# Attention rotations on VectorE from the projection's PSUM bank, the divisor moved into the rotary tables, factor products moved to ScalarE

## The reference, cut to what matters

```python
def apply_partial_rope(t, positions):
    ...
    x1 = tf[..., :half]
    x2 = tf[..., half:ROT_DIM]
    out = jnp.concatenate([x1 * cos - x2 * sin, x2 * cos + x1 * sin, tf[..., ROT_DIM:]], axis=-1)
```

## Time and profile before

| what | value |
|---|---|
| time, median of 3 runs | 2723.34 us (2721.16 to 2724.14) |
| the profiled execution: its own time | 2725.44 us |
| its span, first to last instruction | 2723.6 us |
| mean granted TensorE clock | 0.951 |
| TensorE busy | 2497.2 us (92%) |
| VectorE busy | 1613.0 us (59%) |
| GpSimd busy | 1659.7 us (61%) |
| ScalarE busy | 474.7 us (17%) |

### The profile page before, as it was taken

The page is one execution under the profiler, slowest core; times in us unless marked ns, Lnnn a source line. Parts: engine busy times, 40 slices in busy tenths (PEclk is TensorE's granted clock), DMA queues, the critical chain, the costliest instruction groups (busy, mean ns, idle before and its releaser), DMA issues.

```text
span 2723.6 us, 33885 instructions
## 1 busy us (share of the span) xinstructions
PE 2497.2 (92%) x11937; PEld 2018.0 (74%) x11937; DVE 1613.0 (59%) x1859; ACT 474.7 (17%) x904; POOL 1659.7 (61%) x700
## 2 busy tenths in 40 slices
PE   6998999988999989788888889999999998999997
PEld 4776767866878867677777778878878666887886
DVE  5876234775473377766666647444588565644456
ACT  4523222013000012011101111000032342100000
POOL 4334544665777756455555537787878323777784
PEclk7999999998999989899999999999999888999998
DMA  6212344221323312122222213323323111332331
GB/s 236 70 62 80 118 150 161 102 85 55 112 81 93 113 57 78 62 66 74 66 73 73 65 43 93 96 97 93 107 78 95 54 31 32 93 108 84 94 109 52
DMA packets 61230, 237.70 MB, mean 87 GB/s; under 512 B 7072, under 2 KB 12200, under 8 KB 57424
## 3 DMA queue, kind: packets, MB, share of 16 engines
q1 hardware_dynamic: 54720, 230.51, 26.6%
q10 hardware_dynamic: 6416, 5.95, 0.7%
HBM read 232.24 MB, written 2.10 MB: 86 GB/s over the span
## 4 chain that ended last, share of the span: by engine, by line
PE 76%; DVE 13%; ACT 3%; DVEq 2%; issue 2%; ACTq 1%; POOL 1%; DMA 1%; POOLq 1%
PE gg L533 17%; PE gg L534 17%; PE gg L535 17%; DVE ta L2298 2%; PE babcd L571 2%; PE babcd L573 2%; PE babcd L572 2%; PE gg L907 2%; PE gg L909 1%; PE gg L908 1%; PE babcd L533 1%; PE babcd L534 1%; PE babcd L535 1%; DVEq L2297 1%; DVE qk L2300 1%
## 5 line engine op out<-in xcount | busy, mean ns | idle before, releaser
L463 POOL TENSOR_TENSOR w_hi<-raw,zero 128x1024 fp32r<-128x1024 f32 (+2 forms) x280 | 587.6, 2098 | 687.9 <-PE gg L535 461.7
L465 POOL TENSOR_TENSOR w_lo<-raw,w_hi 128x1024 fp32r<-128x1024 f32 (+2 forms) x280 | 754.0, 2693 | 39.9
L533 PE MATMUL gg<-h_hi,w_hi 128*128 128x512 f32 x1576 | 633.2, 402 | 85.5 <-DVEq L2291 76.0
L534 PE MATMUL gg<-h_lo,w_hi 128*128 128x512 f32 x1576 | 625.2, 397 | 0.0
L535 PE MATMUL gg<-h_hi,w_lo 128*128 128x512 f32 x1576 | 624.7, 396 | 0.0
L533 PEld LDWEIGHTS gg<-h_hi,w_hi 128*128 128x128 f32 x1576 | 304.0, 193 | 161.7 <-DVEq L2291 70.2
L535 PEld LDWEIGHTS gg<-h_hi,w_lo 128*128 128x128 f32 x1576 | 302.8, 192 | 65.4
L534 PEld LDWEIGHTS gg<-h_lo,w_hi 128*128 128x128 f32 x1576 | 304.1, 193 | 62.1
L2024 DVE TENSOR_TENSOR ta<-ff_s,gg 128x512 f32<-128x512 f32 x64 | 44.1, 689 | 331.3 <-PE gg L535 323.8
L454 POOL TENSOR_TENSOR w_hi<-raw,zero 128x1536 fp32r<-128x1536 f32 (+2 forms) x48 | 107.2, 2233 | 186.7 <-PE babcd L535 142.3
L533 PE MATMUL gg<-u_hi,w_hi 128*128 128x512 f32 x528 | 209.7, 397 | 4.2 <-issue 4.2
(11 more groups left out here) (570 smaller groups left out, 3984.3 us busy)
## 6 DMA issues: line engine op xcount, KB each, us to landing
raw<-in_w_ff_in_a SPq DMA_DIRECT2D x66, 512.0 KB, 3.6
raw<-in_w_ff_in_b SPq DMA_DIRECT2D x66, 512.0 KB, 3.6
raw<-in_w_att_qk SPq DMA_DIRECT2D x48, 512.0 KB, 3.6
raw<-in_w_ff_out_a SPq DMA_DIRECT2D x24, 704.0 KB, 4.1
raw<-in_w_ff_out_b SPq DMA_DIRECT2D x24, 704.0 KB, 4.1
late_raw<-in_w_ada SPq DMA_DIRECT2D x16, 1024.0 KB, 5.0
raw<-in_w_ml SPq DMA_DIRECT2D x25, 512.0 KB, 3.6
raw<-in_w_merge_a SPq DMA_DIRECT2D x16, 768.0 KB, 5.5
```

What stands on the lines that cost most here:

```text
L463: pool.tensor_tensor(hi, a, zero[:].to_broadcast([P, size * P]), ALU.add)
L465: pool.tensor_tensor(lo, a, hi, ALU.subtract).then_inc(S["units_split"], 1)
L533: pe.matmul(dst, w_hi[slot][:, blk], xs[0][:, k, :], start=k == 0, stop=False)
L534: pe.matmul(dst, w_hi[slot][:, blk], xs[1][:, k, :], start=False, stop=False)
```

## The change

Four things change, all in the attention.

- `rotate` reads the first 32 rows from the projection's bank instead of from `qk`, and its intermediate results go to bank `bf` (shuffle, cosine product) and to `ta` (sine product). Only head 0's units 2 to 5 still read `qk`. The bank is given back (`att_copied`) by the cosine product, not by the eviction. The eviction still covers all 128 rows, and `rotate` then overwrites the first 32.
- The rotary tables are multiplied by `rstd` once, the first 32 rows of `rstd` become 1, and the second pair of tables goes away. For s below 2, the layout changes in the rotation's sum too.
- In each slot VectorE evicts and rotates unit s first, and the work for the head before comes behind it (`score` at s = 0, `swap_in` at 1, `swap_out` at 2), except `factors`, which stands ahead of unit 3's eviction. TensorE's `att_swap` moves behind unit 2 and writes to `ba`. In head 1 all of this stands one slot later.
- The eight products of `norm` move from VectorE to ScalarE, behind a new semaphore `att_factors`.

Head 0 gets other banks for its units 2 and 5, and another order of evictions.

```diff
@@ -257,12 +257,11 @@
         p_nat = at(62, "p_nat", [P, TB, 2 * P])
         p_res = at(66, "p_res", [P, 4, 2 * P])
         pt_res = at(70, "pt_res", [P, 8 * P])
-        nat_c, nat_s = sq[0][0:32, :], sq[1][0:32, :]
         sel_in = at(95, "sel_in", [P, P])
         sel_out = at(95.5, "sel_out", [P, P])
         rope_c, rope_s = at(80, "rope_c", [32, SEQ]), at(112, "rope_s", [32, SEQ])
         a0, a1, a2 = (at(83 + 2 * i, f"phase{i}", [32, SEQ])[:] for i in range(3))
-        ra = [ta[0:32, :], tb[0:32, :]]
+        ra = ta[0:32, :]
         a_st = at(82, "a_st", [P, 96])
         swap_y = at(82.5, "swap_y", [P, 2, 32])
         swap_m = at(82.875, "swap_m", [P, 2, 4])
@@ -614,7 +613,7 @@
 
                 pe.wait_ge(S["colv_ready"], nth)
                 for b in range(TB):
-                    mm = pe.matmul(bank[:, b:b + 1], rstd[:, b * P:(b + 1) * P], ident[:, 0:1], start=True, stop=True)
+                    mm = pe.matmul(bank[:, b:b + 1], rstd[:, b * P:(b + 1) * P], ident[:, 64:65], start=True, stop=True)
                 mm.then_inc(S["rows_ready"], 1)
 
             def residual(name, kb, xs, nth, shift=False, lead=None, **first):
@@ -1001,9 +1000,7 @@
                 if s < 2:
                     return
                 ready(u0 + s)
-                if s == 5:
-                    pe.wait_ge(S["att_copied"], 2)
-                cols_mm((bf[:], ba, bb, g[1])[s - 2], (u0 + s) % 2, 8, (h_hi, h_lo))
+                cols_mm((bc, ba, bb, bd)[s - 2], (u0 + s) % 2, 8, (h_hi, h_lo))
                 if s == 3:
                     sum_rows(SQ["att"])
                 if s == 5:
@@ -1036,8 +1033,8 @@
                 y = swap_y[:, 0, :].rearrange("p (x r) -> p x r", x=8)
                 for b in range(TB):
                     rows = slice(32 * b, 32 * b + 32)
-                    pe.matmul(bf[rows, 0:8], sel_in[:, rows], y[:, b:8:4, :], start=True, stop=True)
-                pe.matmul(bf[:, 8:40], sel_out[:], swap_y[:, 1, :], start=True, stop=True).then_inc(S["att_swapped"], 1)
+                    pe.matmul(ba[rows, 0:8], sel_in[:, rows], y[:, b:8:4, :], start=True, stop=True)
+                pe.matmul(ba[:, 8:40], sel_out[:], swap_y[:, 1, :], start=True, stop=True).then_inc(S["att_swapped"], 1)
             def att_turn(a):
 
                 for bank, first, last, rows in ((ba, 0, 4, 3), (bb, 4, 7, 4)):
@@ -1070,7 +1067,7 @@
 
                 if s == at_step:
                     att_scores(a, p)
-                if s == at_step + 1:
+                if s == at_step + 2:
                     att_swap(a)
                 if s == 5:
                     att_turn(a)
@@ -1083,7 +1080,7 @@
                             first_head(s)
                             continue
                         project(h, s)
-                        att_step(h - 1, 1 - p, s, 2 * isinstance(h, int))
+                        att_step(h - 1, 1 - p, s, int(isinstance(h, int)))
                     project_values(h, 0)
                     if not first:
                         att_values(h - 1, 1 - p)
@@ -1557,6 +1554,11 @@
             def shifts(a):
                 wait(act, "att_shift", a + 1)
                 act.activation(a_st[:, 40:56], a_st[:, 40:56], ACT.Exp).then_inc(S["att_fexp"], 1)
+            def norm(a):
+                wait(act, "att_factors", a + 1)
+                for n in range(8):
+                    part = p_nat[:, n, nat_part(n)] if n < 4 else p_res[:, n - 4, :]
+                    act.activation(part, part, ACT.Copy, scale=a_st[:, 72 + n:73 + n]).then_inc(S["att_norm"], 1)
             def turned(a):
                 wait(act, "att_values", a)
                 for n, bank in enumerate((ba, bb[:, 0:3 * P], bc, bd)):
@@ -1566,6 +1568,7 @@
             def att_head(a):
                 expo(a)
                 shifts(a)
+                norm(a)
                 turned(a)
             def att_two(i):
                 for p in range(2):
@@ -2275,30 +2278,47 @@
             layer_norm(1, scaled_tile, "att")
             for k in range(KD):
                 add_square(SQ["att"], k)
-            rows_inverse(3)
+            wait(v, "std", 3)
+            v.reciprocal(rstd[:], rstd[:])
             wait(v, "att_consts", 64)
-            v.tensor_copy(by_token(nat_c), by_residue(rope_c[:]))
-            v.tensor_copy(by_token(nat_s), by_residue(rope_s[:]))
             v.drain()
+            v.tensor_tensor(rope_c[:], rope_c[:], rstd[0:32, :], ALU.mult)
+            v.tensor_tensor(rope_s[:], rope_s[:], rstd[0:32, :], ALU.mult)
+            v.drain()
+            v.memset(rstd[0:32, :], 1.0)
+            v.drain().then_inc(S["colv_ready"], 1)
+            def first_bank(s):
+                return (g[0], g[1], bc, ba, bb, bd)[s]
             def projection_out(h, p, s):
 
                 wait(v, "units_used", h * 8 + (FIRST["w_att"] + s + 1))
-                bank = (g[0], g[1], bf[:], ba, bb, g[1])[s] if isinstance(h, int) and h == 0 else g[s % 2]
+                first = isinstance(h, int) and h == 0
+                bank = first_bank(s) if first else g[s % 2]
                 if s < 2:
                     v.tensor_tensor(by_token(qk[p][:, s, :]), by_residue(bank), by_residue(rstd[:]), ALU.mult)
                 else:
-                    v.tensor_tensor(qk[p][:, s, :], bank, rstd[:], ALU.mult)
-                v.drain().then_inc(S["att_copied"], 1)
+                    out = v.tensor_tensor(qk[p][:, s, :], bank, rstd[:], ALU.mult)
+                    if first:
+                        out.then_inc(S["att_copied"], 1)
+                v.drain()
             def rotate(h, p, s):
                 q = qk[p][0:32, s, :]
-                cosine, sine = (nat_c, nat_s) if s < 2 else (rope_c[:], rope_s[:])
-                v.stream_shuffle(ra[0], q, SWAP16)
-                v.tensor_tensor(ra[1], q, cosine, ALU.mult)
-                v.drain()
-                v.tensor_tensor(ra[0], ra[0], sine, ALU.mult)
-                v.drain()
-                v.tensor_tensor(q, ra[0], ra[1], ALU.add)
-                v.drain().then_inc(S["att_roped"], 1)
+                from_qk = isinstance(h, int) and h == 0 and s > 1
+                src = q if from_qk else g[s % 2][0:32, :]
+                turn = bf[0:32, :]
+                v.stream_shuffle(turn, src, SWAP16)
+                v.drain()
+                v.tensor_tensor(ra, turn, rope_s[:], ALU.mult)
+                v.drain()
+                part = v.tensor_tensor(turn, src, rope_c[:], ALU.mult)
+                if not from_qk:
+                    part.then_inc(S["att_copied"], 1)
+                v.drain()
+                if s < 2:
+                    v.tensor_tensor(by_token(q), by_residue(turn), by_residue(ra), ALU.add).then_inc(S["att_roped"], 1)
+                else:
+                    v.tensor_tensor(q, turn, ra, ALU.add).then_inc(S["att_roped"], 1)
+                v.drain()
             def score(a):
 
                 wait(v, "att_turned", a * 4)
@@ -2325,10 +2345,10 @@
             def swap_out(a):
 
                 wait(v, "att_swapped", a + 1)
-                v.tensor_copy(a_st[:, 24:32], bf[:, 0:8])
+                v.tensor_copy(a_st[:, 24:32], ba[:, 0:8])
                 picked = swap_y[:, 1, :].rearrange("p (s r b) -> p s r b", s=2, r=4)
                 for n in range(2):
-                    v.tensor_tensor(picked[:, n, :, :], bf[:, 8 + 16 * n:24 + 16 * n].rearrange("p (r b) -> p r b", r=4),
+                    v.tensor_tensor(picked[:, n, :, :], ba[:, 8 + 16 * n:24 + 16 * n].rearrange("p (r b) -> p r b", r=4),
                                     swap_m[:, 0, :].unsqueeze(2).to_broadcast([P, 4, 4]), ALU.mult)
                 v.drain()
                 tt(picked[:, :, 0:2, :], picked[:, :, 0:2, :], picked[:, :, 2:4, :], ALU.add)
@@ -2346,12 +2366,8 @@
                 tt(eight(64), eight(56), eight(64), ALU.add)
                 v.reciprocal(a_st[:, 64:72], a_st[:, 64:72])
                 v.drain()
-                tt(a_st[:, 72:80], a_st[:, 40:48], a_st[:, 64:72], ALU.mult)
-            def norm(a):
-
-                for n in range(8):
-                    part = p_nat[:, n, nat_part(n)] if n < 4 else p_res[:, n - 4, :]
-                    v.tensor_scalar(part, part, a_st[:, 72 + n:73 + n], None, ALU.mult).then_inc(S["att_norm"], 1)
+                v.tensor_tensor(a_st[:, 72:80], a_st[:, 40:48], a_st[:, 64:72], ALU.mult)
+                v.drain().then_inc(S["att_factors"], 1)
             def head_out(a):
                 wait(v, "att_values", a + 1)
                 hi, lo = (pick(o, a) for o in (o_hi, o_lo))
@@ -2363,50 +2379,33 @@
                 for p in range(2):
                     h = i * 2 + p
                     if isinstance(h, int) and h == 0:
-                        for s in range(6):
+                        for s in (2, 3, 4):
                             projection_out(h, p, s)
-                        for s in range(6):
+                        projection_out(h, p, 0)
+                        rotate(h, p, 0)
```

(42 more changed lines are left out.)

## The result

| | before | after |
|---|---|---|
| median | 2723.45 us (2721.16 to 2724.14, 4 runs) | 2640.71 us (2635.93 to 2643.19, 4 runs) |
| ratio after to before | | 0.9696 [0.9679, 0.9712] |
| profiled execution | 2725.44 us | 2635.93 us |
| span and mean granted clock | 2723.6 us, 0.951 | 2634.1 us, 0.962 |

What follows compares the result with a forecast made beforehand. TensorE was taken as the bound, losing time where it waits for VectorE or runs at half clock. 2725.4 - 103.15 + 15.6 + 1.5 = 2639.3, which stood 2.1 over the median, so 2637 us; range 2617 to 2662.

Steps and rivals of the forecast that it cites:

- What the attention had to give: Attention, head 0's to head 7's value units: 519.86 us against seven full-speed heads of 59.53, so 103.15 us at most.
- VectorE is late because GpSimd holds it: Attention: VectorE operations with both inputs in SBUF wait for GpSimd's instruction, 1878 ns on average against 0.68 us free.
- PSUM as output at no cost: Rotations: writing intermediates to PSUM adds 0, with 0.37 us more as the upper bound.
- D: Rival, rotations: writing PSUM is dearer, 0.2 us on each of fifteen operations ahead of unit 3's bank: 2673; chance 0.08.
- E: Rival, rotations: slower, PSUM reads and writes take turns, near 1 us per operation, ending near 2750; chance 0.03.
- Six waits of 2.6 us before unit 5: Loop heads: GpSimd's splits catch the factors, delaying unit 3's bank; TensorE waits 2.6 us in each of six heads, 15.6.
- rival A: Loop heads: the factors get through ahead of GpSimd's split, no wait before unit 5: 2621; chance 0.27.
- no clock loss: Behind the 2.6 us wait before unit 5, the granted clock holds at 1.00.
- rival C: Loop heads: the clock falls behind the new wait, costing 3.0 us in each of six heads: 2655; chance 0.15.
- Head 1 at 1 us: Head 1: factors one slot later delay no bank; the transposes wait for ScalarE's products, 1 us.
- The start at 0, give or take 1: Head 0: the 2.59 us wait goes, value units begin 5.44 and some behind unit 4 either way: 0.
- The order hides its parts: Slots 0 and 1: score operations and `swap_in` fit behind the rotations, hidden under TensorE's units; the exchange finds its input ready.

Runs made afterwards that it cites:

- all_three: The changed kernel with factors behind unit 3's rotation in every head, head 1 in the loop's order, and head 0's unit 5 evicted first: 2616.56 us.
- order_only: The kernel before with the new slot order and the products on ScalarE, its own rotation kept in SBUF: 2681.74 us.
- temp_sbuf: The changed kernel with the rotation's shuffle and cosine product written to an SBUF tile instead of bank bf: 2678.26 us.
- products_vector: The changed kernel with the eight products back on VectorE, between the factors and unit 3's eviction: 2705.6 us.
- after_again: The changed kernel run once more, unaltered, on another chip: 2637.51 us.
- evict_first: The changed kernel with head 0's unit 5 evicted ahead of unit 0's eviction and rotation, TensorE waiting for that: 2629.98 us.
- scalar_only: The kernel before with the eight products moved to ScalarE and nothing else: 2692.79 us.
- old_order: The changed kernel with the slot order of before in the loop's heads, rotation and ScalarE products kept: 2642.46 us.
- factors_late: The changed kernel with the factors behind unit 3's rotation in the loop's heads, instead of ahead of its eviction: 2628.67 us.

## Why the prediction was right

**What the attention had to give: right for this change.** 103.15 us at most, against full-speed heads of 59.53: the change took 87.6 of it, and all_three 102.4. The words "without waits" were wrong: each such head holds up to 1 us of wait for ScalarE's copy of the transposes, which the change doesn't touch.

**VectorE is late because GpSimd holds it: right, but drawn too narrow.** order_only, temp_sbuf and the change differ in where the operands lie and in next to nothing that adds work, and they stand at 2681.7, 2678.3 and 2640.7. What I left out is that a product with one tensor input is held as well (products_vector). It did not enter the sum, since the products went to ScalarE, but it is why that part of the change was needed beside the new order.

**PSUM as output at no cost: right**, 687 ns against 679. Rivals D and E needed 0.2 and 0.6 us more. Their counts were too high: of the fifteen operations that they charge, only eight write PSUM (shuffle and cosine product of four slots), so by writing alone E would have needed (14.7 - 5.6) / 8 = 1.1 us; and the 14.7 that it starts from is a mean over seven heads in which head 1 had 21.5. At 8 ns neither matters. The rule of 65 ns more for a PSUM source, which the prediction weighed against it (the Trainium skill, VectorE: DVE Perf Modes, on the TRN2 errata), doesn't show here: the sine product takes 679 ns with one source in PSUM, and took 0.68 us with both in SBUF and GpSimd still.

**Six waits of 2.6 us before unit 5, 15.6 in all: the mechanism and the size right, the count wrong, the clock wrong.** The marks came as clocked: counted from unit 2's end (1166.66 in head 2), the factors were forecast at 5.9 and came at 5.82, GpSimd's split at 6.06 and came at 6.07. Two heads of six had the wait, at 2.47 (the prediction's own marks, 14.0 against 11.5, give 2.5); four got through as in rival A. I had put the margin at 0.2 us with start marks no better than 0.1, and it was that fine: that four heads won was not foreseen. Where the wait did come, the step "no clock loss" failed: it rested on one row at 2.59 us, and behind 2.47 the clock fell, which is rival C at about 1.65 us a head, not 3.0, since it was soon back. Why heads 2 and 3 of all heads lose is known in part. In head 3 an operation of `swap_out` begins 0.40 us late without a wait that the profile shows, and the factors start at 6.03 instead of 5.71:

```profile
1235.40 0.17 DVE L1704 TENSOR_TENSOR a_st<-swap_y 128x8 f32<-128x8 f32 x1 [0.40 <-issue]
```

In head 2 ScalarE's exponential still starts at 5.40, as in head 4, and the factors behind it 0.1 us later than there. Both are so in after_again and evict_first too. The two heads are the first pass through the loop; whether that makes the delays is not shown.

**Head 1 at 1 us: wrong, it was 5.84.** I let its factors run free because they delay no bank. But one slot later they meet the splits of 12 blocks. VectorE's timeline there, and ScalarE's behind it:

```profile
1112.58 2.99 DVE L1704 TENSOR_TENSOR a_st<-a_st 128x8 f32<-128x8 f32 x2
...
1115.92 3.26 DVE L2369 TENSOR_TENSOR a_st<-a_st 128x8 f32<-128x8 f32 x1
```

```profile
1119.24 1.60 ACT L1561 ACTIVATE p_nat<-p_nat,a_st 128x128 f32<-128x128 f32 x4 [6.78 <-DVEq L2370]
1120.75 1.69 ACT L1561 ACTIVATE p_res<-p_res,a_st 128x256 f32<-128x256 f32 x4
```

So ScalarE begins at 1119.24, and the transposes wait 2.41 us; some 2 us behind that the granted clock falls to 0.50. In all_three this head has the loop's order, and its transposes don't wait.

**The start at 0, give or take 1: wrong, it was 2.6.** I said the value units began "5.44 and some" behind unit 4 either way. They began at 1061.76, 0.2 from where they were (1061.95), so that was right; but the wait of 2.59 that went had left the clock at 1.00, and the one of 2.67 in its place did not. The sum had counted the wait and not what follows it. Which of the two follows was not to be read from that one row: in scalar_only, which has the same code up to there, the same wait came out at 2.57 us, and the lower clock did follow, while in order_only it was 2.56 and the clock stayed at 1.00. TensorE's timeline in scalar_only, and the window behind it with the columns of the earlier trace rows:

```profile
1057.35 0.76 PE L533 MATMUL gg<-h_hi,w_hi 128*128 128x512 f32 x1 [2.57 <-DVEq L2297]
```

```profile
1057.40:1061.00 3.60, 3.60 (x10) 2.85 (x11) 2.08 (x3) 0.00 (x0) 3.46 (x2) 0.58 0.02 7
```

**ScalarE's products at most 4.0 us:** 1.60 and 1.69, so 3.3, and hidden but for head 1. In head 7's tail I had taken 0.5, and 0.35 came. **The order hides its parts:** right in that no slot-0 or slot-1 wait came; but the expectation that it was needed for the gain fell with old_order, and the place that it gives the factors, ahead of unit 3's eviction, cost 9.6 us from mark to mark (432.24 against 422.60 in factors_late).

**The sum** was close in part by luck, because its errors offset: 15.6 + 1.0 in the heads were forecast and 15.5 came, 4.35 and 4.39 from two heads, 5.84 from head 1, 0.95 from the other four. The start's +2.6 and the -4.8 of scatter behind head 7's finish offset as well.

## What to carry to other kernels

Where VectorE shares its time with GpSimd, ask of each operation whether it has two tensor inputs in SBUF, or one in a fast fp32 form, and what GpSimd does at that moment: the same eight products cost 3.0 us on average in one slot and 8.6 in the next, and a free PSUM bank for intermediates was worth 37 us. Put short operations that GpSimd can hold behind the one that gives back a bank, not ahead of it. And build the floor of a stage from its undisturbed units first: it told before any run how much this change could win. Look inside such a unit for waits as well: here 6.8 us of them stayed in the floor and out of sight.
